# A four-layer transformer kernel on one core: modulation rows in quarters of the array, first weights rounded ahead of x, gelu products as jobs of the projection, weight chunks fetched further ahead

## The reference, cut to what matters

```python
def ada_chunks(cvec, w, b):
    m = jax.nn.silu(cvec) @ w + b
    return jnp.split(m[..., None, :], 6, axis=-1)

def modulate(x, g, shift, scale):
    return rms_norm(x, g) * (1 + scale) + shift

def chunk_gmlp(u, v, w_s, b_s, g_v):
    bn, length, _ = u.shape
    u = jax.nn.gelu(u)
    v = layer_norm(jax.nn.gelu(v), g_v)
    v = v.reshape(bn, length // A_CHUNK, A_CHUNK, A_GROUPS, A_GDIM)
    s = jnp.einsum('gij,bnjgc->bnigc', w_s, v) + b_s.T[None, None, :, :, None]
    return u * s.reshape(bn, length, A_WIDTH)
...
        xm = modulate(h, g_pre_m, sh_m, sc_m)
        cm = modulate(hc, g_pre_m, csh_m, csc_m)
...
        y_a = chunk_gmlp(u, va, w_s, b_s, g_v)
        y_b = neighbourhood_attention(q, k, vb, kc, vbc, rpb)
        y = jnp.concatenate([y_a, y_b], axis=-1) @ w_out
```

## Time and profile before

| | |
|---|---|
| median of 3 runs | 4423.28 us (4421.26 to 4425.78) |
| profiled execution | 4422.46 us, span 4420.7 us |
| mean granted TensorE clock | 0.935 |
| busy TensorE (PE) | 3896.3 us, 88% |
| busy VectorE (DVE) | 2089.4 us, 47% |
| busy ScalarE (ACT) | 1448.8 us, 33% |
| busy GpSimd (POOL) | 1546.3 us, 35% |

### The profile page before, as it was taken

The page is one execution under the profiler, slowest core; times in us unless marked ns, Lnnn a source line. Parts: engine busy times, 40 slices in busy tenths (PEclk is TensorE's granted clock), DMA queues, the critical chain, the costliest instruction groups (busy, mean ns, idle before and its releaser), DMA issues. The chain is left out here.

```text
span 4420.7 us, 51623 instructions
## 1 busy us (share of the span) xinstructions
PE 3896.3 (88%) x18724; PEld 3021.0 (68%) x18724; DVE 2089.4 (47%) x3587; ACT 1448.8 (33%) x2238; POOL 1546.3 (35%) x756
## 2 busy tenths in 40 slices
PE   6777889999788879999998677899999988778999
PEld 3775678888666658867886443688778866337887
DVE  4817877443545675645445756322232232552222
ACT  2216232222326533333223254322232233443222
POOL 1221134444130135543553211355444532104454
PEclk8989999999989989999999887999999998789999
DMA  6430124442110136744662110133322321102332
GB/s 206 144 76 18 56 95 133 140 134 63 34 43 1 37 105 211 229 137 152 219 226 78 48 33 1 53 96 97 92 77 90 100 74 54 29 1 67 95 95 72
DMA packets 459779, 409.76 MB, mean 93 GB/s; under 512 B 30063, under 2 KB 404975, under 8 KB 459631
## 3 DMA queue, kind: packets, MB, share of 16 engines
q1 hardware_dynamic: 457183, 406.50, 30.1%
q10 hardware_dynamic: 2448, 1.32, 0.1%
HBM read 404.10 MB, written 7.60 MB: 93 GB/s over the span
## 5 line engine op out<-in xcount | busy, mean ns | idle before, releaser
L198 POOL TENSOR_TENSOR s_wlo<-s_raw,s_whi 128x1024 fp32r<-128x1024 f32 x490 | 1180.9, 2417 | 2233.6 <-ACT s_whi L190 2233.2
L212 PE MATMUL psum<-s_xhi,s_whi 128*128 128x512 f32 x3264 | 1239.9, 380 | 121.3 <-DVE s_xlo L421 69.5
L213 PE MATMUL psum<-s_xlo,s_whi 128*128 128x512 f32 x3264 | 1230.8, 377 | 0.0
L214 PE MATMUL psum<-s_xhi,s_wlo 128*128 128x512 f32 x3264 | 1225.5, 375 | 0.0
L190 ACT ACTIVATE s_whi<-s_raw 128x1024 fp32r<-128x1024 f32 x490 | 508.8, 1054 | 1809.2 <-PE psum L214 1753.3
L212 PEld LDWEIGHTS psum<-s_xhi,s_whi 128*128 128x128 f32 x3264 | 621.7, 190 | 251.3 <-issue 135.8
L213 PEld LDWEIGHTS psum<-s_xlo,s_whi 128*128 128x128 f32 x3264 | 621.6, 190 | 114.7 <-issue 4.5
L214 PEld LDWEIGHTS psum<-s_xhi,s_wlo 128*128 128x128 f32 x3264 | 620.0, 190 | 114.4
L212 PE MATMUL psum<-s_ahi,s_whi 128*128 128x512 f32 x1232 | 481.3, 391 | 32.8 <-POOL s_wlo L198 22.7
L213 PE MATMUL psum<-s_alo,s_whi 128*128 128x512 f32 x1232 | 472.8, 384 | 0.0
L214 PE MATMUL psum<-s_ahi,s_wlo 128*128 128x512 f32 x1232 | 472.4, 383 | 0.0
(11 more groups left out here) (229 smaller groups left out, 4288.4 us busy)
## 6 DMA issues: line engine op xcount, KB each, us to landing
s_ada_raw<-w_ada SPq DMA_DIRECT2D x224, 512.0 KB, 3.8
s_raw<-w_gu SPq DMA_DIRECT2D x176, 512.0 KB, 3.9
s_raw<-w_up SPq DMA_DIRECT2D x88, 512.0 KB, 4.7
s_raw<-w_dn SPq DMA_DIRECT2D x88, 512.0 KB, 3.5
s_raw<-w_down SPq DMA_DIRECT2D x44, 512.0 KB, 4.6
s_raw<-w_in SPq DMA_DIRECT2D x28, 512.0 KB, 3.9
s_raw<-w_in_ab SPq DMA_DIRECT2D x20, 512.0 KB, 6.1
s_area<-w_first SPq DMA_DIRECT2D x16, 512.0 KB, 11.9
```

Source lines behind the costliest of these rows:

```text
L198: pool.tensor_tensor(K.wlo[:, c % HL, 0:a * b], K.raw[:, c % RAW, 0:a * b], K.whi[:, c % HL, 0:a * b].bitcast(F32), ALU.subtract).then_inc ...
L212: pe.matmul(out, lh, rh, start=first, stop=False)
L213: pe.matmul(out, lh, rl, start=False, stop=False)
L214: return pe.matmul(out, ll, rh, start=False, stop=last)
```

## The change

- `FirstNorm`: the Silu of c is written 16 times (32 columns for each k) into a tile `first_c`; each of the 32 matmuls has 32 stationary columns and writes 32 partitions of bank 2; four in a row, for the two groups and the two halves of 512, go to different quarters of the array. The chunks come in the order k, t. One copy of 128 x 512 takes all out; the transposing matmuls read quarter by quarter.
- ScalarE rounds weight chunks 0 and 1 in `FirstNorm`, after that copy and ahead of `high`, and chunk 2 in `Begun` as before.
- Class `U` is gone. Its four products are jobs 8 to 11 of the q and k projection, with the gelu at their read-out into t1 and t2 (`gated`). `GmlpMix` multiplies by them, on VectorE, one group behind the mixing.
- `Proj.sp` fetches chunk c0 + i + 5 in step i, and not c0 + i + 3, where a projection has modulation tasks. That is this one projection alone.
- In the first attention, SP issues the first four bias loads ahead of the raw chunks that `ahead` fetches.

```diff
--- before.py
+++ after.py
@@ -231,7 +231,10 @@
         for dst, src in K.early:
             e.dma_start(dst, src).then_inc(K.sem["early_in"], 16)
         e.wait_ge(K.sem["cols_in"], 16)
-        e.activation(K.ada_sum[:, :], K.cols[:, COLS["c"]:COLS["c"] + 16], ACT.Silu).then_inc(K.sem["first_silu"], 1)
+        c = K.cols[:, COLS["c"]:COLS["c"] + 16].rearrange("p (k v) -> p k v", v=2)
+        for i in range(16):
+            ins = e.activation(K.first_c[:, :, 2 * i:2 * i + 2], c, ACT.Silu)
+        ins.then_inc(K.sem["first_silu"], 1)
         e.wait_ge(K.sem["early_in"], 16 * len(K.early))
 
     def dve(self, e):
@@ -291,7 +294,7 @@
         e.dma_start(K.rpb_rows, K.io["rpb"].unsqueeze(1).to_broadcast([120, GRID, P])).then_inc(K.sem["rpb_in"], 16)
 
     def act(self, e):
-        for c in range(HL):
+        for c in range(2, HL):
             split_hi(self.K, e, c)
 
     def pool(self, e):
@@ -530,68 +533,73 @@
         super().__init__(K, T, None, pre)
 
     def counts(self):
-        n = len(self.tasks)
         c = super().counts()
-        c.update(first_used=8 * n, first_row=n, first_col=n)
+        c.update(first_used=8 * len(self.tasks), first_row=1, first_col=1)
         return c
 
     def sp(self, e):
-        K = self.K
-        for c in range(8 * len(self.tasks)):
+        K, n = self.K, len(self.tasks)
+        for c in range(8 * n):
             if c >= FIRST:
                 e.wait_ge(self.sem["first_used"], c - FIRST + 1)
-            t, k = divmod(c, 8)
+            k, t = divmod(c, n)
             e.dma_start(K.ada_first[:, c % FIRST, :], K.io["w_first"][k * P:(k + 1) * P, t * D:(t + 1) * D]).then_inc(
                 K.sem[f"first_rows{c % FIRST}"], 16)
 
-    def rows(self, t):
-        return self.K.pf[0:2, (2 + 2 * t) * BANK:(4 + 2 * t) * BANK]
-
-    def columns(self, t):
-        return self.K.pf[:, (6 + t) * BANK:(6 + t) * BANK + 16]
+    def rows(self, j):
+
+        return self.K.pf[32 * j:32 * j + 32, 2 * BANK:3 * BANK]
+
+    def columns(self, j):
+        return self.K.pf[:, (4 + j) * BANK:(4 + j) * BANK + 8]
 
     def pe(self, e):
-        K = self.K
+        K, n = self.K, len(self.tasks)
         super().pe(e)
         e.wait_ge(K.sem["first_silu"], 1)
-        for c in range(8 * len(self.tasks)):
-            t, k = divmod(c, 8)
+        for c in range(8 * n):
+            k, t = divmod(c, n)
             e.wait_ge(K.sem[f"first_rows{c % FIRST}"], 16 * (c // FIRST + 1))
-            for a in range(0, D, BANK):
-                ins = e.matmul(self.rows(t)[:, a:a + BANK], K.ada_sum[:, 2 * k:2 * k + 2],
-                               K.ada_first[:, c % FIRST, a:a + BANK], start=(k == 0), stop=(k == 7))
+            for a in range(2):
+                ins = e.matmul(self.rows(2 * t + a), K.first_c[:, k, :],
+                               K.ada_first[:, c % FIRST, a * BANK:(a + 1) * BANK], start=(k == 0), stop=(k == 7))
             ins.then_inc(self.sem["first_used"], 1)
-        for t in range(len(self.tasks)):
-            e.wait_ge(self.sem["first_row"], t + 1)
-            for m in range(8):
-                ins = e.matmul(self.columns(t)[:, 2 * m:2 * m + 2], K.ada_raw[0:2, t, m * P:(m + 1) * P], K.ident[0:2, 0:2],
-                               start=True, stop=True)
-            ins.then_inc(self.sem["first_col"], 1)
+        e.wait_ge(self.sem["first_row"], 1)
+        for m in range(4):
+            for j in range(2 * n):
+                r = slice(32 * j, 32 * j + 2)
+                ins = e.matmul(self.columns(j)[:, 2 * m:2 * m + 2], K.ada_raw[r, 0, m * P:(m + 1) * P],
+                               K.ident[r, 32 * j:32 * j + 2], start=True, stop=True)
+        ins.then_inc(self.sem["first_col"], 1)
 
     def h_there(self, act, k):
         act.wait_ge(self.K.sem["x_in"], 32)
 
     def act(self, e):
-        K = self.K
+        K, n = self.K, len(self.tasks)
         self.squares(e, 0, K.h, self.h_there)
         for dst, src in K.consts:
             e.dma_start(dst, src).then_inc(K.sem["const_in"], 16)
-        for t in range(len(self.tasks)):
-            e.wait_ge(self.sem["first_used"], 8 * t + 8)
-            e.activation(K.ada_raw[0:2, t, :], self.rows(t), ACT.Copy).then_inc(self.sem["first_row"], 1)
+        e.wait_ge(self.sem["first_used"], 8 * n)
+        e.activation(K.ada_raw[0:64 * n, 0, 0:BANK], K.pf[0:64 * n, 2 * BANK:3 * BANK],
+                     ACT.Copy).then_inc(self.sem["first_row"], 1)
+        for c in range(2):
+            split_hi(K, e, c)
         self.high(e)
 
     def dve(self, e):
         K = self.K
         e.wait_ge(K.sem["x_in"], 32)
         self.rsqrt(e, 0)
+        e.wait_ge(self.sem["first_col"], 1)
         for t, dst in enumerate(self.tasks):
-            e.wait_ge(self.sem["first_col"], t + 1)
             b = COLS["b_ada"] + 8 * t
+            cols = K.pf[:, (4 + 2 * t) * BANK:(6 + 2 * t) * BANK].rearrange("p (j c) -> p j c", j=2)
             for v in range(2):
-                ins = e.tensor_tensor(K.mod[:, dst[v]:dst[v] + 8], self.columns(t)[:, v::2], K.cols[:, b:b + 8], ALU.add)
-            ins.then_inc(K.sem["dve_step"], 1)
-            e.wait_ge(K.sem["dve_step"], K.step())
+                ins = e.tensor_tensor(K.mod[:, dst[v]:dst[v] + 8].rearrange("p (j c) -> p j c", j=2), cols[:, :, v:8:2],
+                                      K.cols[:, b:b + 8].rearrange("p (j c) -> p j c", j=2), ALU.add)
+        ins.then_inc(K.sem["dve_step"], 1)
+        e.wait_ge(K.sem["dve_step"], K.step())
         for s in range(2):
             self.gains(e, s)
         self.low(e)
@@ -728,7 +736,7 @@
     def sp(self, e):
         self.ahead(e)
         for i in range(self.n):
-            load_chunk(self.K, e, self.c0 + i + HL)
+            load_chunk(self.K, e, self.c0 + i + (RAW - 1 if self.ada.tasks else HL))
             for g, q in self.rows_at(i):
                 self.ada.load(e, g, q)
 
@@ -1147,20 +1155,31 @@
 
 class GmlpMix(Phase):
 
+
+    def __init__(self, K, gated):
+        self.gated = gated
+        super().__init__(K)
+
     def counts(self):
-        return self.ring_counts(T0, 4)
+        c = self.ring_counts(T0, 4)
+        c.update(ya_done=4)
+        return c
 
     def dve(self, e):
         K = self.K
         nt = T0 // P
-        for g in range(4):
-            e.wait_ge(self.sem["out_ready"], self.at("out_ready", g + 1))
-            src = self.slot(T0, g).rearrange("p (n i) -> p n i", n=nt)
-            bs = K.b_s[:, g * P:(g + 1) * P].unsqueeze(1).to_broadcast([P, nt, P])
-            ins = e.scalar_tensor_tensor(out=K.sT[:, g, :].rearrange("p (n i) -> p n i", n=nt), in0=src,
-                                         scalar=K.cols[:, COLS["a_v_g"] + g:COLS["a_v_g"] + g + 1], in1=bs,
-                                         op0=ALU.mult, op1=ALU.add)
-            ins.then_inc(self.free(T0, g), 1)
+        for i in range(5):
+            if i < 4:
+                e.wait_ge(self.sem["out_ready"], self.at("out_ready", i + 1))
+                src = self.slot(T0, i).rearrange("p (n i) -> p n i", n=nt)
+                bs = K.b_s[:, i * P:(i + 1) * P].unsqueeze(1).to_broadcast([P, nt, P])
+                e.scalar_tensor_tensor(out=K.sT[:, i, :].rearrange("p (n i) -> p n i", n=nt), in0=src,
+                                       scalar=K.cols[:, COLS["a_v_g"] + i:COLS["a_v_g"] + i + 1], in1=bs,
+                                       op0=ALU.mult, op1=ALU.add).then_inc(self.free(T0, i), 1)
+            if i > 0:
+                g = i - 1
+                e.wait_ge(self.free(T0, g), self.is_read(T0, g))
+                e.tensor_tensor(K.sT[:, g, :], K.sT[:, g, :], self.gated[g], ALU.mult).then_inc(self.sem["ya_done"], 1)
 
     def pe(self, e):
         K = self.K
@@ -1292,7 +1311,8 @@
 
     def sp(self, e):
         K, bias = self.K, self.bias
-        self.ahead(e)
+        if not bias or bias.raws < 4:
+            self.ahead(e)
         if not bias:
             return
         e.wait_ge(K.sem["ada_read"], self.ada_read)
@@ -1300,6 +1320,8 @@
         e.wait_ge(self.sem["bias_kept"], self.at("bias_kept"))
         e.wait_ge(self.sem["qn_ready"], self.at("qn_ready"))
         for i in range(bias.n):
+            if i == bias.raws:
+                self.ahead(e)
             if i >= bias.raws:
                 e.wait_ge(self.sem["e_ready"], self.at("e_ready", i - bias.raws + 1))
                 if bias.raws == 4:
@@ -2028,9 +2050,9 @@
         + [f"ada_in{i}" for i in range(2)] + [f"e_in{i}" for i in range(4)] + EXTRA_SEMS)
 
 
-def copy_to(dst, rows=slice(None), scale=1.0):
-
-    return lambda e, src: e.activation(dst, src[rows], ACT.Copy, scale=scale)
+def copy_to(dst, rows=slice(None), scale=1.0, func=ACT.Copy):
+
+    return lambda e, src: e.activation(dst, src[rows], func, scale=scale)
 
 
 def tokens_to(dst, col, func=ACT.Copy):
@@ -2147,6 +2169,7 @@
         Start(K)
 
         mods = [(L0X + 8 * g, L0C + 8 * g) if g < 8 else (L0X + 8 * g,) for g in range(12)]
```

(55 more changed lines are left out.)

## The result

The changed kernel takes 4386.51 us (median of 4 runs, 4381.07 to 4391.33), the kernel before 4422.75 beside it (4 runs): ratio 0.9914, 95% interval 0.9901 to 0.9927. Forecast were 4385.5 us, in a range of 4371 to 4400. So the gain is 36.2 us by these medians (0.9%, clear of the noise), where 37.8 were forecast.

The account below looks back on a forecast made before the run. VectorE's serial chain, its head waiting for `pos`, and TensorE's class U stage were taken to bound the start: v projections 40.2 us sooner, less a 2.4 us cold start, is 37.8; 4423.3 - 37.8 = 4385.5 us, range 4371 to 4400.

Parts of the forecast that it names:

- The large term: Ahead of the v projections: gelu products as jobs take the class U stage off the path, 34.0 us less there.
- Nine jobs at 8.4 us without a gap: TensorE's q and k projection: jobs 3 to 11 run gapless from 142 to 220 us, behind a stop of some 17.
- Part 1: Modulation rows at the start: matmuls in four array quarters run at once, rows end at 40 us instead of 55.6.
- Part 2: Chunks 0 and 1 rounded ahead of x, by 44.5 us; `low` ends at 67 us instead of 78.2.
- Where DVE's chain starts: VectorE's casts and bias table: the cast waits for `pos`, and the table ends 10 us sooner, near 127.
- a table's end off by over 4 us: Sign at the bias table's end, forecast near 127 us: missing it by more would make the prediction wrong.
- The 24 chunks: VectorE's modulation chunks beside the projection: six more raw loads at about 1.0 us each make 80.8 us into 86.8.
- A: Rival at VectorE's chain start: `pos` isn't held back, the table ends at 117.4, 47 us saved, 4376; chance 0.12.
- B: Rival at VectorE's modulation chunks: raw transfers slow them to 95 us for 24, 29 us saved, 4394; chance 0.15.
- C: Rival at the modulation rows: quarters don't overlap, rows end at 55.6, 27.8 us left, 4395.5; chance 0.08.
- D: Rival at the modulation rows: no overlap and a lower array clock, rows end at 92, slower, 4431.5; chance 0.03.
- E: Rival behind the early gains: an unseen wait on SP or ScalarE gives some back, 4398 to 4415; chance 0.12.

Follow-up runs that it names:

- The run without parts 1 and 2: The changed kernel with the modulation rows and the first weights' rounding as before, its jobs and SP's order kept: 4389.63 us, ratio 0.9926.
- those two parts alone: The kernel before with only the modulation rows in quarters and chunks 0 and 1 rounded ahead of x: 4419.18 us, ratio 0.9993.
- the near fetch: The changed kernel with raw chunks fetched three steps ahead, as before, not five: 4386.17 us, ratio 0.9910.
- SP's old order: The changed kernel with SP's bias loads put back behind the products' early weight loads, as before: 4386.72 us, ratio 0.9916.

## Why the prediction was right, and where it wasn't

**The large term** is right in place and size. From the chunks' end to the first maximum 34.0 us less were forecast (103.8 to 69.8) and 36.4 measured. The run without parts 1 and 2 has 31.4 of the 36.2 us, those two parts alone 1.9, and the near fetch and SP's old order lose nothing: what counts is that the gelu products are jobs. The mixing took 7.3 us (7 forecast). The 2.4 left over are a cold start that the forecast charged to the v projections a second time. They have one in both kernels: TensorE stopped ahead of them and was then granted a clock of 0.58 from 271.9 to 276 us before, and of 0.54 from 234.3 to 238 after, which is for the most part the lower level of 1.2 GHz, so the 42.8 us that they took before held that loss already, and after they took 42.4, not 45.2.

```profile
271.89 0.36 PE L212 MATMUL psum<-s_whi,s_xhi 128*128 128x256 f32 x1 [2.11 <-ACT s_t L2433]
```

```profile
234.34 0.51 PE L212 MATMUL psum<-s_whi,s_xhi 128*128 128x256 f32 x1 [2.22 <-DVE s_area L1176]
```

Nine jobs at 8.4 us without a gap are right. The stop ahead of them has the length forecast (18.05 us, forecast 17), but both its ends came 7 to 8 us late (149.64, forecast 142), with the table. TensorE's stop of 12.5 us until 85.10 was missed, and the first projection's last read came at 105.26, where the projection was to end near 99; that cost nothing, since TensorE stood further on anyway.

**Part 1** is right. Four quarters run at once: in the last groups, where only one chunk is there and its two halves use two quarters, four records take 1.05 us (0.26 each), while 48 over all four take 5.36 (0.11 each). The rows end at 39.5 (forecast 40), behind the transfers. The Trainium skill, "TensorE: Matmul & The Clock Gate", section "Measured speedup vs the span model", has 2.38 times for three column tiles. Here it is 0.43 / 0.112 = 3.8 times for four, nearer to the number of tiles, and the measurement decides. The run without parts 1 and 2 shows the old cost of the small transposes too, in its TensorE timeline; in quarters they take 1.07 us:

```profile
55.66 3.73 PE L567 MATMUL psum<-s_ident,s_ada_raw 2*128 2x2 f32 x32
```

**Part 2** nearly so: chunk 1 was split at 45.77 and not by 44.5, so `low` stood 3.4 us for ScalarE's high half, but it still ended at 64.9 (forecast 67).

**"Where DVE's chain starts" failed in two of its three terms.** Forecast: 2.6 us from `pos`, 3.4 from the casts, 4.0 from the table, 10 in all. Measured: -3.4, +1.2 and +4.0, 1.7 in all with the rounding. By the prediction's own sign ("a table's end off by over 4 us") this step is wrong: 135.6 against 127. The reading that `pos` decides once x is early was right, and the run with `pos` first shows it; before the change x and `pos` came together, and the cast stood for neither. But `pos` was priced by the start of the queue; it lands 0.5 to 1.7 us behind `rpb_rows`, which took 28.5 to 33.9 us from issue to landing in the profiles, whatever was edited. Among the kernels with x early that leave SP's order here alone, `pos` landed between 77.0 and 82.6, and the forecast had bounds of 75 and 79. And the casts met GpSimd again because `dve = pool = _wait` holds GpSimd for the same transfer and frees both at once (82.77 and 82.70); I had read only VectorE's wait. The run with GpSimd free gives back 2.6 to 3 us. The two early splits were moved away from the table, and that saved 4.0 as forecast.

**The 24 chunks** were to take 86.8 us and took 80.9. The 6 us added for more raw loads lie within a scatter that the forecast didn't have: over all profiles with two buffers and full work the stretch was 79.2 to 86.8, with the same 48 operations and 11 to 16 us of waits for `w_ada`. What differs is how much of GpSimd's subtractions VectorE's operations met. Summed over L352's rows, the excess over 1.22 us is 10.5 us in the changed kernel (11 rows stretched) and 15.5 in the one with the bias loads last (12 rows), whose chunks take 86.8: 48 x 1.22 + 10.5 + 12.0 = 81.1 and 48 x 1.22 + 15.5 + 12.8 = 86.9. So it hangs on how the two engines' operations fall in time, and up to 6 us of any result here come from it. All 11 stretched rows are operations with both inputs in SBUF; the 24 with one input in PSUM keep their 1.22 us. The Trainium skill, "SBUF — State Buffer", section "SBUF: two separate sides", calls the port pair of VectorE and GpSimd an exclusive lock, held for a whole instruction; the trace agrees: the longest excess of any profile, 2.2 us, is just under one subtraction of 2.4.

**The rivals.** A wanted a `pos` that isn't held (it took 33.4 us), B chunks of 95 us (80.9), C and D quarters that don't overlap (0.112 us a record), E a time of 4398 or more: none came.

That the total was met to 1.6 us (gains of 36.2 and 37.8) is in part luck: three misses cancel, the table 8.3 us late against the plan, the chunks 5.9 and the rest 2.4 us short of it. That is no merit of the sum. What stays open is why `rpb_rows` took 28.5 us in one profile and 33.9 in another; with one profile for each program, it can't be told whether that goes with the program or with the execution. Nor was the swap of `pos` run without the early x; before, the cast at 80.58 hadn't stood for `pos`, so the swap alone should gain little, but that is argued and not shown.

## What to carry to other kernels

Work made faster at the head of a kernel is worth nothing until the wait that ends last there moves: here x was ready 13 us sooner, and VectorE then stood 15.5 us for a 256 KB load, queued behind one of 3840 KB; with x early, swapping the two brought the first maximum 11.8 us forward. Before a wait is priced, look up in the code which other engines wait for the same thing, since what they do when freed falls on the first instructions behind it. When two engines end a stage together, relieving one, or the other, shows nothing; relieve both, and look for what then bounds them (here a two-buffer loop), since only that told of the third. And before a difference of a few us is put down to an edit, look at how far stretches that nobody edited differ between profiles (here 6 us for the same 24 chunks).

## What the hardware showed that wasn't expected

Four 32-column fp32 matmuls of 512 columns in four quarters took about as long as one of before: 0.112 us a record against 0.43. 32 transposing matmuls of two rows fell from 3.73 to 1.07 us. The copy of `rpb` from memory to memory, 3840 KB (3.93 MB), ran at 116 to 138 GB/s from issue to landing (33.9 and 28.5 us), while the loads at 27 to 38 us had 305 GB/s, and a load behind it in SP's queue was held until it had ended, though from 72 to 78 us the transfer engines were busy for a share of 0.24 only. A small load ahead of it took 5.4 us, and the copy took no longer for that (28.5 us).
